# A decoder trunk with split-precision matmuls: the RMS scale of a token applied at the exit from PSUM, the token rows split tile by tile

## What is computed

```
def rmsnorm(x, g):
    xf = x.astype(jnp.float32)
    y = xf * lax.rsqrt(jnp.mean(xf * xf, axis=-1, keepdims=True) + EPS)
    return (y * g.astype(jnp.float32)).astype(x.dtype)

def conv_ffn(xn, buf, w_up, conv_w, conv_b, w_down):
    u = xn @ w_up
    g, v = u[..., :D_FF], u[..., D_FF:]
    gc, new_buf = causal_dwconv(g, buf, conv_w, conv_b)
    return (jax.nn.gelu(gc) * v) @ w_down, new_buf.astype(buf.dtype)

x = x + conv_ffn(rmsnorm(x, f_norm), ...)          # both layers
kv = rmsnorm(x, kv_norm) @ w_kv + b_kv             # after the first
```

## Time and profile before

| | us |
|---|---|
| median of 3 runs | 2624.71 (2623.25 to 2625.06) |
| profiled execution | 2623.81 |
| its span | 2622.0 |
| TensorE matmuls busy | 2494.7 (95%), clock granted 0.976 of full |
| VectorE / ScalarE / GpSimd busy | 1199.3 (46%) / 855.9 (33%) / 285.5 (11%) |

### The profile page before, as it was taken

How to read it: one execution, slowest core, us unless ns; L and a number is a source line. 1 busy time by engine, 2 the same in 40 slices (tenths; PEclk the granted TensorE clock), 3 DMA queues, 4 the chain that set the end, 5 groups by cost and what they waited for, 6 DMA issues and landing times.

```text
span 2622.0 us, 39675 instructions
## 1 busy us (share of the span) xinstructions
PE 2494.7 (95%) x15088; PEld 2417.9 (92%) x15088; DVE 1199.3 (46%) x1882; ACT 855.9 (33%) x1495; POOL 285.5 (11%) x388
## 2 busy tenths in 40 slices
PE   5999889999999999999999889989999999999998
PEld 4899888999999999999988855989999999999998
DVE  7566555533343333333386776264323333433432
ACT  3455432431331232122244476133213313311211
POOL 2011323000000000000321054230000000000000
PEclk7999989999999999999999998999999999999999
DMA  3111111111111111111152310101111111111112
GB/s 111 41 41 40 30 40 36 40 42 46 48 40 40 55 41 36 52 48 32 48 76 45 93 54 1 41 25 53 36 56 40 42 46 48 38 42 48 48 36 84
DMA packets 222513, 121.95 MB, mean 47 GB/s; under 512 B 24541, under 2 KB 220061, under 8 KB 222332
## 3 DMA queue, kind: packets, MB, share of 16 engines
q1 hardware_dynamic: 220180, 117.18, 15.4%
q10 hardware_dynamic: 2196, 3.74, 1.2%
q0 software_dynamic: 64, 0.05, 0.0%
HBM read 112.30 MB, written 10.55 MB: 47 GB/s over the span
## 4 chain that ended last, share of the span: by engine, by line
PE 82%; DVE 8%; issue 3%; ACT 3%; DMA 2%; POOL 1%; SPq 0%; ACTq 0%; DVEq 0%; POOLq 0%
PE ps L692 26%; PE ps L694 26%; PE ps L693 26%; PE ps L968 1%; DMA raw<-in_w_q 1%; PE ps L1020 1%; DVE nlo L1518 1%; DVE rstd L1487 1%; DVE convin L1510 1%; DVE y L1510 1%; DVE wlo L1482 1%; PE ps L865 1%; ACT whi L1090 0%; ACT nhi L1111 0%; DVE nlo L1918 0%
## 5 line engine op out<-in xcount | busy, mean ns | idle before, releaser
L692 PE MATMUL ps<-nhi,whi 128*128 128x384 f32 (+1 forms) x3312 | 1098.6, 332 | 63.5 <-POOL nlo L1951 25.0
L694 PE MATMUL ps<-nhi,wlo 128*128 128x384 f32 (+1 forms) x3312 | 1088.9, 329 | 0.0
L693 PE MATMUL ps<-nlo,whi 128*128 128x384 f32 (+1 forms) x3312 | 1088.2, 329 | 0.0
L692 PEld LDWEIGHTS ps<-nhi,whi 128*128 128x128 f32 x3312 | 628.1, 190 | 83.5 <-issue 67.9
L693 PEld LDWEIGHTS ps<-nlo,whi 128*128 128x128 f32 x3312 | 628.7, 190 | 1.6 <-issue 0.2
L694 PEld LDWEIGHTS ps<-nhi,wlo 128*128 128x128 f32 x3312 | 628.2, 190 | 0.0
L1482 DVE TENSOR_TENSOR wlo<-raw,whi 128x1024 fp32r<-128x1024 f32 (+2 forms) x220 | 244.8, 1113 | 622.6 <-ACT whi L1090 622.6
L694 PE MATMUL ps<-hhi,wlo 128*128 128x384 f32 (+1 forms) x1152 | 376.0, 326 | 0.0
L692 PE MATMUL ps<-hhi,whi 128*128 128x384 f32 (+1 forms) x1152 | 375.8, 326 | 0.0
L693 PE MATMUL ps<-hlo,whi 128*128 128x384 f32 (+1 forms) x1152 | 375.7, 326 | 0.0
L1090 ACT ACTIVATE whi<-raw 128x1024 fp32r<-128x1024 f32 (+2 forms) x220 | 208.3, 947 | 447.9 <-PE ps L694 440.2
(11 more groups left out here) (281 smaller groups left out, 2018.4 us busy)
## 6 DMA issues: line engine op xcount, KB each, us to landing
raw<-in_f_w_up SPq DMA_DIRECT2D x96, 512.0 KB, 3.8
raw<-in_f_w_down SPq DMA_DIRECT2D x64, 384.0 KB, 3.5
raw<-in_a_w_in SPq DMA_DIRECT2D x16, 512.0 KB, 4.0
xrows<-in_x_prompt SPq DMA_DIRECT2D x8, 512.0 KB, 6.4
raw<-in_a_w_out SPq DMA_DIRECT2D x8, 512.0 KB, 4.1
raw<-in_w_q SPq DMA_DIRECT2D x16, 256.0 KB, 3.7
raw<-in_w_o SPq DMA_DIRECT2D x32, 128.0 KB, 3.0
strip<-strip_sb ACTq DMA_DIRECT2D x1, 3072.0 KB, 32.9
```

The costliest lines, as they stand in the source:

```text
L692: pe.matmul(out, whi[s][:, w], mhi[:, k, chunk(c)], start=(k == 0), stop=False)
L693: pe.matmul(out, whi[s][:, w], mlo[:, k, chunk(c)], start=False, stop=False)
L694: last = pe.matmul(out, wlo[s][:, w], mhi[:, k, chunk(c)], start=False, stop=(k == nk - 1))
```

## The change

- The input of both feed-forwards' up projections and of keys and values is gain x x, without rstd. For tiles 0 to 5 ScalarE rounds the whole tile right after its squares, and VectorE subtracts right after its weight pass; for tiles 6 and 7 both go chunk by chunk (`last_residual`).
- rstd is multiplied in where results leave PSUM, on VectorE: `rescaled` takes banks 0 to 2 to convin (before: ScalarE), y is multiplied by rstd after gelu, and `kv_out` takes keys and values. ScalarE adds their bias in a pass of its own (`biased`).
- The sums over channels for chunks 1 and 2 go into the first pair, behind the second input tile of the first side's pieces. The first pair still alternates chunk by chunk, and now waits by `split_done`.
- Two regions, sa and sb with 12 tiles each and sc4 with 4, take the place of nhi, nlo, hhi, hlo, so that the new split can be written while the old input is still read. The norm ahead of the queries stays as it was.

```diff
 # TensorE
+            def split_done(p, v=None):
+                def before(c, k):
+                    if (c, k) == (0, 0):
+                        pe.wait_ge(xs_lo, xs_tiles(p) + FB)
+                    if k == FB:
+                        pe.wait_ge(xs_lo, xs_tiles(p) + FB + 2 * (c + 1))
+                    if v is not None and k == 2 and c < 2:
+                        stats(v, c + 1)
+                return before
...
-                if v:
-                    stats(v, 1)
...
-                        piece(n, s, c, KD, nhi, nlo,
-                              None if s else first_piece if v == 0 and c < 2 else normed(u))
-                        if (c, s) == (0, 1) and v:
-                            stats(v, 2)
+                        piece(n, s, c, KD, m, None if s else first_piece if v == 0 and c < 2 else ready)
...
-                        first_pair(nb, u, v)
+                        first_pair(nb, m, None, v, None, split_done(p, v))
 # ScalarE
+            def residual(n, i, v, gain, big, last_cols, phase):
                 for s in range(2):
                     for c in range(3):
+                        squared(n, i, v, s, c)
+                    kt = 2 * i + s
+                    act.activation(big[:, ds(kt, 1), :], x[:, ds(kt, 1), :], ACT.Copy, scale=pcol[:, ds(kt, 1), gain])\
+                       .then_inc(xs_hi, 1)
+                    prep(n + 1, s, last_cols, phase)
+            def last_residual(n, v, gain, m, last_cols, phase):
...
+                squared(n, i, v, 1, 0)
+                highs(0)
+                root(v, 0)
+                squared(n, i, v, 1, 1)
+                highs(1)
+                prep(n + 1, 1, last_cols, phase)
+                squared(n, i, v, 1, 2)
+                root(v, 1)
+                highs(2)
+                root(v, 2)
...
-                        evac_conv(0, n, 2, 2 * (KD + f), KD + f)
                         prep(n + 1, 0, next_cols, phase)
...
+            def biased(m, s):
+                act.wait_ge(bank_free[3 * s + 2], N_KV + m + 1)
+                bias_s = pcol[:, 2 * m + s, C_BKV:C_BKV + 1]
+                if m == 0:
+                    act.activation(kf[:, s, KS:KT], kf[:, s, KS:KT], ACT.Identity, bias=bias_s).then_inc(kv_biased, 1)
+                    keys = blocks(kf[:, s, 0:KS])[:, :, 1:KB]
+                    act.activation(keys, keys, ACT.Identity, bias=bias_s).then_inc(kv_biased, 1)
...
             for s in range(2):
-                for c in range(3):
-                    kv_out(0, s, c)
                 prep(N_KV + 1, s, KD * P)
+                biased(0, s)
+                act.wait_ge(kv_biased, 2 * s + 2)
...
+            for s in range(2):
+                biased(1, s)
             states_to_dram(0)
 # VectorE
+            def last_residual(n, v, p, gain, m, next_cols, bias_col=None):
...
+                added(n, i, 1, 0, bias_col)
+                lows(0)
+                recip(v, 0)
+                added(n, i, 1, 1, bias_col)
+                lows(1)
+                added(n, i, 1, 2, bias_col)
+                prep(n + 1, 1, next_cols)
+                recip(v, 1)
+                lows(2)
+                recip(v, 2)
+                seq.settle()
...
+            def rescaled(n):
+                gp, gs = sp_view(convin, FFN_W - 1)
+                for c in range(3):
+                    dve.wait_ge(bank_ready[c], n + 1)
+                    lo, w = CHUNKS[c]
+                    if c == 2:
+                        w = SEQ - lo
+                        dve.tensor_tensor(gs[:, :, FFN_W - 1:], requests(ps[:, c, w:w + NS]), requests(rstd[:, SEQ:T]),
+                                          ALU.mult)
+                    dve.tensor_tensor(gp[:, FFN_W - 1 + lo:FFN_W - 1 + lo + w], ps[:, c, 0:w], rstd[:, lo:lo + w], ALU.mult)\
+                       .then_inc(bank_free[c], 1)
...
                         dve.wait_ge(gelu_done, g + 1)
+                        seq.mark(dve.tensor_tensor(y[:, :], y[:, :], rstd[:, :], ALU.mult))
+                        seq.settle()
...
+            for c in range(3):
+                for s in range(2):
+                    kv_out(0, s, c)
...
             for c in range(3):
                 for s in range(2):
-                    dve.wait_ge(bank_ready[3 * s + c], N_Q)
-                norm(3, C_BN, None, [c], lambda k: prep(N_Q, 0, KD * P) if (c, k) == (0, 6) else None)
+                    kv_out(1, s, c)
+                norm(1, C_BN, None, [c], split_b, lambda k: prep(N_Q, 0, KD * P) if (c, k) == (0, 6) else None)
```

362 lines of the change are left out of this document (193 added, 169 removed).

## The result

| | before | changed |
|---|---|---|
| median of 4 runs each | 2623.98 (2622.85 to 2625.06) | 2592.61 (2588.96 to 2592.98) |
| ratio, with its 95% interval | | 0.9877 (0.9860 to 0.9894) |
| profiled execution, its span | 2623.81, 2622.0 | 2592.98, 2591.0 |
| TensorE matmuls busy, clock granted | 2494.7, 0.976 | 2486.1, 0.978 |
| VectorE / ScalarE / GpSimd busy | 1199.3 / 855.9 / 285.5 | 1304.0 / 783.1 / 244.1 |

The change saves 31.4 us, 1.2%; forecast were 34.3 and a time of 2590.4 us. That is six times the 5 us that the prediction took as the least a measurement can tell.

What follows compares the result with a forecast made beforehand. TensorE sets the pace in the loop, and each stage start costs about 14 us over its work, waiting for normed tokens. 12.7 + 10.8 + 14.1 - 3.3 = 34.3 us gained, giving 2590.4 us; range 2584 to 2600.

Steps and rivals of the forecast that it cites:

- The three starts: First tile pairs of both feed-forwards and keys/values: token scale leaves the matmul input, gaining 12.7, 14.1 and 10.8 us.
- (b): Rival: stage starts keep a third of their cost, each sum waiting for a VectorE reciprocal; 12 us less gain, 2602; chance 0.09.
- (d): Rival: the split of tiles 0 to 5 is late, TensorE waits at its first matmul, nothing won; 2625; chance 0.01.
- no low part of tokens but in the query stage: Sign of being right: TensorE's table of waits shows low parts of tokens only in the query stage.
- Loop tiles at 0: 48 feed-forward tiles: 3.0 us more on VectorE costs 0, covered by 1.8 us ahead of the product with bank 5.
- Rival (c): VectorE becomes late in the loop and each of 48 tiles pays; at 1.0 a tile 2638; chance 0.04.
- 8.9 us for the next weights: Feed-forward loop: cover for the next weights, ready at 511.2 and wanted at 520.1.
- Rounding the whole tile: Residual tiles 0 to 5: one ScalarE pass of about 1.1 us beside units of 11.9 or 8.9 us, called free.
- Keys and values to queries: From the key/value pair's end to the query sums: 1.5 + 1.0 + 0.85, 3.3 us lost.
- rival (e): The key/value part hides wholly; 2587; chance 0.10.
- the exits' term of 1.85: Keys/values to queries: two more VectorE exits ahead of each chunk of norms, 1.0 and for the last chunk 0.85.
- Rival (a): Query weights lose the race with the strip; the even tile starts some 5 us later; 2593 to 2597; chance 0.14.

Runs made afterwards that it cites:

- Experiment 4: Changed kernel, but VectorE takes the reciprocal of chunk 0 behind the last residual add and subtractions of chunk 1; 2588.61 us in one run.
- Experiment 5: Changed kernel with the scale still at the exit, but all 8 tiles split chunk by chunk at the stage start, none ahead of time; 2590.31 us.
- experiment 6: Changed kernel with one more VectorE pass over y ahead of the multiplication by rstd in each of the 48 up tiles; 2590.81 us.
- experiment 2: Changed kernel, but ScalarE's queue sends the bias strip as soon as it is copied, ahead of the key/value pair's end; 2586.95 us.

## Why the prediction was right, point by point

- **The three starts.** Forecast 24.9, 26.85 and 24.9; measured 24.89, 26.90 and 24.91. The order of VectorE's queue, laid on the durations of the earlier trace rows, gave the waits at the new sums to 0.1 us: none at the feed-forwards, 1.1 for a forecast 1.0 at keys and values. Experiment 4 shows that it is the reciprocal. That the sums of the feed-forward starts don't wait was forecast with a margin of 0.1 us and came with 0.2, less than such a sum of durations can promise: there luck has a part. Rivals (b) and (d) fell here: no pair keeps a third of its cost, and the first matmul doesn't wait. Experiment 5 shows the limit of this: with another order the same wait is there from the table load.
- **Who held up the starts.** The prediction read the earlier trace rows as if both rows, 25.0 and 16.2 us, belonged to the starts. Only GpSimd's do, 23.1 of 25.0; VectorE's seven waits lie in the norm ahead of the recurrent block. Its sum doesn't use them, so nothing came of it, but its sign "no low part of tokens but in the query stage" could not come true as written.
- **Loop tiles at 0.** Measured 831.52 for 831.57 and 851.54 for 851.66, VectorE at 17.3 for a forecast 17. The cover of 1.8 us read as 1.81 and took another pass in experiment 6. Rival (c) would have needed much more: four further passes cost no tile inside a block anything, but for the one behind the first pair. One cover was read too large, without harm: 8.9 us for the next weights holds in the loop, behind the first pair it is 1.9 for the odd side. VectorE's exits of 384 columns took 557 ns each (96 of them), as the adds had.
- **Rounding the whole tile: the step that failed.** The prediction laid it beside units of 11.9 or 8.9 us and called it free. That is so in all pairs but the first of the output projection. There TensorE has only 36 matmuls to do behind a wait of 9.9 us, and the next weights are wanted as soon as they can be made: before, the next matmul started 1.04 us behind the last of these. Every instruction of ScalarE ahead of the weight pass is on the path there, and the new one was 1.19 us long. The prediction looked for queues that the pass stands in at the feed-forward's start, not at the start of the loop that it was added to. Price 1.1, and 1.6 more where the lower clock follows, as in the profiled execution.
- **Keys and values to queries.** Forecast 3.3 lost, measured from the end of the pair to the query sums 65.61 - 63.08 = 2.5, and 1.0 more at the lower clock behind, which the prediction had as a bound (1.7) and not in the sum. So rival (e) fell. The place was right, one term too large. The strip went out at 2.6 behind the pair's end, forecast 2.5, but the odd weights were picked up 0.9 later than before (36.55 for 35.64), not 1.5. The strip landed 2.1 later (35.96 for 33.89), but the odd weights no longer so far behind it, 0.6 in place of 1.7: they were issued 0.4 and 1.3 us behind the strip, before 2.2 and 2.6, and moved packets beside it from the start (last section). From this pick-up to the issue of the states' DMAs it takes 1.6 more (21.66 for 20.03), which is the exits' term of 1.85. That the bias passes wouldn't hold up the issue of the states is in the rows:

```profile
1378.73 1.21 ACT L1378 ACTIVATE t<-t,pcol 128x1088 f32<-128x1088 f32 x1 [1.10 <-POOL sc L2058]
1378.79 0.56 ACTq L1348 DMA_DIRECT2D out_ffn_conv_p<-fout  x1
```

- **Rival (a).** The even query weights did not lose the race: they were issued ahead of the strip, 1322.49 and 1322.91 for 1323.22. Where experiment 2 made them lose, they took up to 25.7 us and still cost nothing.
- **The sum.** Forecast 34.3, measured 31.0 between the spans: 37.6 gained at the starts for 37.6 forecast, less 2.2 (no term), less 3.5 with its clock (3.3), less 0.9 in the attention (no term). The gain was right to 0.1 and the losses were set too low by 3.3: the pass 1.1, what else is different ahead of the first feed-forward 1.1 (the lower clock 1.6, less 0.5 for the earlier start), the clock behind the query sums 1.0 and the attention 0.9, less 0.8 for the strip. All but the pass and the strip differ between executions. An execution of the changed kernel at 2588.96 and one at 2592.98 stand in the same series.

What stays open: why the span up to the first feed-forward lies anywhere between 431.8 and 437.3 in kernels that are the same up to 363 us, and do so by 3.5 us at that place already (358.7 to 362.2). That the differences come and go with stretches at the lower clock is likely and not shown, and no edit was made against them.

## What to carry to other kernels

A factor that depends only on the token and comes late (a norm's scale) belongs behind the matmul: what it cost ahead of it was 11 to 14 us at each stage start, and in the loop it costs nothing behind it, since the engine that applies it has idle time at that point of the tile, which the trace shows in one bracket. Where that engine has none, between keys and values and the queries, it cost 2.5. Ask of a pass that is added to a loop what stands behind it in the first iteration, where nothing is ahead to hide it. A large transfer that nobody waits for should go out behind the small ones that somebody does: here one DMA moved by 4 us gave 3.8 us.

## What the runs showed of the hardware

- A DMA that is issued behind a large one on another queue shares with it at once, or not for a long time. With the strip early, the first two query loads were issued at 1320.73 and 1321.14, 8.4 and 8.8 us behind it. In the window 1320.8 to 1335 only the strip's queue (q10) moved data:

```profile
q10 hardware_dynamic: 947, 1.45, 88.8%
```

  and from 1338 to 1344 both queues did, packet for packet, 1536 bytes for 256:

```profile
q10 hardware_dynamic: 400, 0.61, 88.5%
q1 hardware_dynamic: 396, 0.10, 7.5%
```

  In the changed kernel the odd loads were issued 0.4 and 1.3 us behind the strip, and from 1328 to 1332 they already moved packets beside it:

```profile
q10 hardware_dynamic: 263, 0.40, 88.2%
q1 hardware_dynamic: 183, 0.05, 5.1%
```

  In the kernel before they came 2.2 and 2.6 us behind it, and from 1347 to 1360 their queue moved nothing. The Trainium skill, DMA: Bandwidth & Descriptors, Queues, rings and completion order, has the engines alternate between the queues at packet granularity. By that rule the windows in which both move are as they should be. For the empty ones it says nothing as long as the second queue had no packets ready, and whether it had no trace shows. What they do show is that the issuing queue itself is held: the second and third issue took 5.2 and 16.9 us with the strip early, against 0.4 to 0.9 for all four with the strip late. Why 0.4 us of lag and 2.2 differ so is open.
- Sharing packet for packet is a bad deal for the small packets: the query loads got 7.5% of the engines' time beside 88.5% for the strip. 256 KB took 28 to 33 us in the changed kernel, and 25 with the strip early (14 of them without a packet), in place of 3 to 4.
- Alike waits of TensorE are followed by the lower clock in some executions and not in others. At 363 us it was idle for 1.92 us in the three that then fell, for 1.77 to 1.82 in three that did not, and for 0.70 to 0.97 in six that did not either. Ahead of the first query sums it was idle for 2.5 to 2.8 us in eleven of the twelve kernels: six of them went on at the lower clock for a while, the changed one among them (2.76 us of idle time), and five did not (2.74 to 2.78). So the length of the wait alone doesn't settle it.
